# Late keys scored from transposed rows on TensorE, a swept input projection, a re-ordered bank queue and an interleaved cross-attention in a one-layer hybrid decoder step

## The reference, cut to what matters

```python
h = rmsnorm(x); q, k, v, u = split(h @ w_in)         # q,k,v: 8 heads x 64; u: 512 channels
# mixer A, prompt: dilated window attention among the 256 tokens, with a bias by distance
# mixer A, sample: 4 new queries against a cache of 2048 keys, three branches
#   (window, dilation) = (128,1), (512,4), (2048,16); branches merged by their softmax denominators
# mixer B: trailing means over 2/4/8/16 positions minus the token, one 128x128 map per group
x += concat(A, B) @ w_out
mk, mv = rmsnorm(mem) @ w_xk, rmsnorm(mem) @ w_xv    # 256 memory rows for the prompt
x += softmax(q_x @ keys) @ values @ w_xo             # 4 heads x 256; each sample has its own cached 256 rows
x += moe(rmsnorm(x))                                 # top 4 of 32 experts, each 1024 -> 2048 -> 1024
y = rmsnorm(x)                                       # and the caches, shifted by 4 rows, are outputs
```

## Time and profile before

| | |
|---|---|
| median of the runs | 1447.03 us (1445.16 to 1451.53, 3 runs) |
| the profiled execution | 1451.07 us, of which its span is 1449.3 us |
| mean granted TensorE clock | 0.953 of full speed |
| busy, us | PE 1274.4, PEld 530.7, DVE 479.3, ACT 238.5, POOL 67.2 |
| moved by DMA | 562.83 MB, mean 388 GB/s |
| the chain that ended last | DMA 49%, PE 38%, DVE 10%, issue 1%, ACT 1% |

### The profile page before, as it was taken

The page is one execution under the profiler, slowest core; times in us unless marked ns, Lnnn a source line. Parts: engine busy times, 40 slices in busy tenths (PEclk is TensorE's granted clock), DMA queues, the critical chain, the costliest instruction groups (busy, mean ns, idle before and its releaser), DMA issues.

```text
span 1449.3 us, 16480 instructions
## 1 busy us (share of the span) xinstructions
PE 1274.4 (88%) x6397; PEld 530.7 (37%) x6397; DVE 479.3 (33%) x1020; ACT 238.5 (16%) x467; POOL 67.2 (5%) x69
## 2 busy tenths in 40 slices
PE   7985978899779799999999899899998999989996
PEld 4352333347554433333333333333332333333332
DVE  2038989631413523122221231213212222123124
ACT  2135343220221111100010011011010001001102
POOL 1010000002202400000000000000000000000000
PEclk9985988799999699999999999999999999999999
DMA  9979698799989999999999999999999999999993
GB/s 352 360 257 365 252 384 349 290 352 377 339 311 391 336 395 430 427 428 426 427 429 430 429 427 429 430 428 428 428 428 430 428 427 428 430 429 427 428 428 141
DMA packets 51212, 562.83 MB, mean 388 GB/s; under 512 B 6501, under 2 KB 8645, under 8 KB 20349
## 3 DMA queue, kind: packets, MB, share of 16 engines
q1 hardware_dynamic: 49589, 557.16, 94.1%
q0 software_dynamic: 1584, 5.13, 0.9%
HBM read 556.15 MB, written 73.28 MB: 434 GB/s over the span
## 4 chain that ended last, share of the span: by engine, by line
DMA 49%; PE 38%; DVE 10%; issue 1%; ACT 1%; SPq 0%; DVEq 0%
DMA wide<-in_w_gate_up 48%; PE bank L1816 11%; PE bank L1511 3%; PE bank L1400 3%; PE bank L1532 3%; PE bank L1845 2%; PE bank L1554 2%; PE bank L1618 2%; DVE small L1120 2%; DVE wide L1117 1%; PE bank L1416 1%; DMA wide<-in_cache_mem_k 1%; PE bank L1669 1%; DVE wide L1118 1%; PE bank L1798 1%
## 5 line engine op out<-in xcount | busy, mean ns | idle before, releaser
L1816 PE MATMUL bank<-wide,att 128*64 128x512 f32 x2048 | 463.7, 596 | 60.5 <-DMA wide<-in_w_gate_up 60.3
L1816 PEld LDWEIGHTS bank<-wide,att 128*64 128x64 f32 x2048 | 139.1, 136 | 365.1 <-issue 228.0
L1845 PE MATMUL bank<-slim,att 128*64 128x512 f32 x1024 | 226.8, 595 | 0.0
L1322 DVE TENSOR_SCALAR att<-bank 128x512 f32<-128x512 f32 x32 | 22.1, 691 | 471.4 <-PE bank L1816 471.4
L1845 PEld LDWEIGHTS bank<-slim,att 128*64 128x64 f32 x1024 | 70.6, 137 | 152.2 <-issue 149.2
L1301 DVE TENSOR_TENSOR x<-x,bank 128x512 f32<-128x512 f32 x68 | 46.6, 685 | 233.0 <-PE bank L1798 226.4
L920 ACT ACTIVATE att<-att 128x512 f32<-128x512 f32 x32 | 20.2, 630 | 520.0 <-DVE att L1322 520.0
L1798 PE MATMUL bank<-tb,att 128*128 128x512 f32 (+1 forms) x192 | 84.7, 611 | 1.8 <-issue 1.3
L929 ACT ACTIVATE tb<-bank 64x512 f32<-64x512 f32 x64 | 37.8, 591 | 234.1 <-PE bank L1845 233.7
L1532 PE MATMUL bank<-slim,ta 128*128 128x512 f32 x128 | 58.2, 608 | 0.0
L1120 DVE TENSOR_REDUCE small<-wide 128x24 f32<-128x1536 f32 x32 | 56.1, 1753 | 1.1
(11 more groups left out here) (271 smaller groups left out, 1131.8 us busy)
## 6 DMA issues: line engine op xcount, KB each, us to landing
wide<-in_w_gate_up SPq DMA_DIRECT2D x128, 2048.0 KB, 25.5
slim<-in_w_down SPq DMA_DIRECT2D x64, 2048.0 KB, 22.0
out_k_win_sample<-in_cache_k_win SPq DMA_DIRECT2D x16, 2044.0 KB, 24.3
out_v_win_sample<-in_cache_v_win SPq DMA_DIRECT2D x16, 2044.0 KB, 29.0
wide<-in_cache_k_win SPq DMA_DIRECT2D x16, 1024.0 KB, 9.6
wide<-in_cache_v_win SPq DMA_DIRECT2D x16, 1024.0 KB, 6.8
wide<-in_w_in SPq DMA_DIRECT2D x8, 1024.0 KB, 14.8
wide<-in_cache_mem_k SPq DMA_DIRECT2D x8, 1024.0 KB, 19.7
```

The lines of the kernel that those rows point to most:

```text
L1816: ins = M(bk[half[h], :], rows[:, k, :], wide[:, k, c:c + 512], start=False, stop=k == KC - 1)
L1845: ins = M(bank_y[half[h], :], aT[:, f % 4, f // 4, :], slim[:, f, 512 * h:512 * h + 512], start=f == 0, stop=f == KC - 1)
```

## The change

It has four parts that share one diff.

**Late keys.** Slot 8 is no longer multiplied on DVE. TensorE transposes it (job `trl b`), ACT evicts it (`lateT`), TensorE multiplies it with `qd`, in which each query stands in its own head's 64 rows and zeroes elsewhere (job `sl b`, four matmuls of 8 columns), and DVE adds the bias from PSUM straight into the score tile. DVE builds `qd` once.

**Projection sweep.** `u` and tile 0's q, k, v are done together chunk by chunk in seven banks; then the bias products, `state`, the eight `toep`, `qkv 2`, `utp`, `uts`, and last tile 1. ACT and DVE follow in that order, so that the trailing sums come while tile 1 is multiplied.

**Re-ordered queue.** SP loads `x` before `ident` and `gcol`, and the weights before the bias constants. The first key and value windows wait for job `qkv 1 2` and no longer stand behind the load of `diag`, which waits for `stored["pool"]`. `COPIES` is now 6 and 4 around the bias load, 2 after the windows, 1, 0, 1, 1, 1 in the loop, 2 after it, 2 behind the cached memory keys, then 5, 2, 2 as before, and 3 instead of 6 behind the first expert's `w_gate_up`.

**Cross-attention.** `qm` is zeroed before the residual and filled one `xq` job at a time. The list `CROSS` interleaves the sample keys and scores with the prompt units; `xpt 3` and `xo_ 3` come after `xpts`.

```diff
-        add("bias_w"), add("bias_f")
+        for c in range(4):
+            add("u", c)
+        for c in range(3):
+            add("qkv", 0, c)
+        add("bias_w"), add("bias_f"), add("state")
+        for h in range(HEADS):
+            add("toep", h)
+        add("qkv", 2), add("utp"), add("uts")
+        for c in range(3):
+            add("qkv", 1, c)
...
-        COPIES = [7, 2, 1, 1, 1, 1, 1, 1, 2, 5, 2, 2, 6]
+        COPIES = [6, 4, 2, 1, 0, 1, 1, 1, 2, 2, 5, 2, 2, 3]
...
-            add("qb", b, 2), add("pt", b)
+            add("qb", b, 2), add("sl", b), add("pt", b)
...
+            if b + 1 < DEC_B:
+                add("trl", b + 1)
...
+        CROSS = [("keys", 2), ("scores", 1), ("xs", 0), ("keys", 3), ("scores", 2), ("xs", 1), ("xpt", 0), ("keys", 4), ("scores", 3),
+                 ("xo_", 0), ("keys", 5), ("scores", 4), ("xs", 2), ("xpt", 1), ("keys", 6), ("scores", 5), ("xo_", 1), ("keys", 7),
+                 ("scores", 6), ("xs", 3), ("scores", 7), ("xpt", 2), ("xo_", 2)]
...
 # SP
-            sp.wait_ge(stored["pool"], 48)
-            load(sp, "diag", own, i["c_diag"])
-            b, use = place(("u", 3))
+            b, use = place(("qkv", 1, 2))
             sp.wait_ge(bank_full[b], use + 1)
             window(kwin[0], i["cache_k_win"], 0, k_in[0])
             window(vwin, i["cache_v_win"], 0, v_in)
             window(kwin[1], i["cache_k_win"], 1, k_in[1])
+            sp.wait_ge(stored["pool"], 48)
+            load(sp, "diag", own, i["c_diag"])
...
 # ACT, after the fills of a turn
+            def late_turned(b):
+                ps, s = product(act, "trl", b)
+                if b:
+                    b_, use = place(("sl", b - 1))
+                    act.wait_ge(bank_full[b_], use + 1)
+                A(lateT, ps[:, :].rearrange("p (c n) -> p c n", n=P), ACT.Copy).then_inc(s, 1)
...
 # DVE, in the loop over b and t
-                dve.wait_ge(late_k, b + 1)
-                    V.tensor_tensor(prod[:, 0:2, :], pair, ps[:, :].unsqueeze(1).broadcast_to([P, 2, AW]), ALU.mult)
-                    V.tensor_tensor(prod[:, 2, :], kw[:, 8, :], ps[:, :], ALU.mult).then_inc(s, 1)
+                    V.tensor_tensor(prod, pair, ps[:, :].unsqueeze(1).broadcast_to([P, 2, AW]), ALU.mult).then_inc(s, 1)
-                    link(V.tensor_reduce(S_[b % 2][:, :, t, :], prod.rearrange("p k (h d) -> p k h d", d=HD), AX.X, ALU.add))
+                    link(V.tensor_reduce(S_[b % 2][:, 0:2, t, :], prod.rearrange("p k (h d) -> p k h d", d=HD), AX.X, ALU.add))
                     if b and t < 3:
                         (shift, sums, shares)[t](b - 1)
+                    if t == 2:
+                        ps, s = product(dve, "sl", b)
+                        V.tensor_tensor(S_[b % 2][:, 2].rearrange("p t (c h) -> p c t h", h=2),
+                                        ps[:, 0:32].rearrange("p (c t h) -> p c t h", c=4, h=2),
+                                        bsw[:, 2].rearrange("p t (c h) -> p c t h", h=2), ALU.add).then_inc(s, 1)
...
 # TensorE: row(b, 2), then late_scores(b), then turned(b); late_turn(b + 1) after the fills
+            def late_turn(b):
+                pe.wait_ge(late_k, b + 1)
+                ps, s = take(pe, "trl", b)
+                for c in range(4):
+                    ins = TR(ps[:, P * c:P * c + P], kwin[b % 2][:, 8, P * c:P * c + P], ident[:, :])
+                ins.then_inc(s, 1)
+            def late_scores(b):
+                read_out(pe, "trl", b)
+                ps, s = take(pe, "sl", b)
+                for c in range(4):
+                    ins = M(ps[:, 8 * c:8 * c + 8], lateT[:, c, :], qd[:, c, 8 * b:8 * b + 8], start=True, stop=True)
+                ins.then_inc(s, 1)
...
 # DVE, qm
-            for b in range(DEC_B):
-                ins = V.tensor_copy(qm.rearrange("p (c b n) -> p c b n", c=KC, b=DEC_B)[:, :, b, DEC_T * b:DEC_T * b + DEC_T],
-                                    tb[:, :, SEQ + DEC_T * b:SEQ + DEC_T * b + DEC_T])
+            for c in range(8):
+                read_out(dve, "xq", c)
+                V.tensor_copy(qm[:, QB * c:QB * c + QB].rearrange("p (b n) -> p b n", b=DEC_B)[:, :, 0:DEC_T],
+                              tb[:, c, SEQ:T].rearrange("p (b t) -> p b t", t=DEC_T)).then_inc(qm_in, 1)
```

More of the change, by code:

```diff
@@ L730, in _, with rows_out @@
                 root(t, n, x[0:n, t, :], hn[0:n, t, :])
[L732 to L735, removed]
+            def rows_out(t):
                 for c in range(3):
@@ L738, in _ @@
                     A(qkvn[:, c, t, :], ps[:, :], ACT.Copy, scale=HD ** -0.5 if c == 0 else 1.0).then_inc(s, 1)
-            ps, s = product(act, "qkv", 2)
-            for c in range(3):
-                ins = A(qkvn[0:NS, c, 2, :], ps[NS * c:NS * c + NS, :], ACT.Copy, scale=HD ** -0.5 if c == 0 else 1.0)
-            ins.then_inc(s, 1)
             for c in range(4):
@@ L747, in _ @@
                 A(uS[:, c, :, STATE:US], ps[:, SEQ:T].rearrange("p (b t) -> p b t", t=DEC_T), ACT.Copy).then_inc(s, 1)
+            rows_out(0)
+            ps, s = product(act, "state")
+            A(uS[:, :, :, 0:STATE], ps[:, 0:480].rearrange("p (g b n) -> p g b n", g=4, n=STATE), ACT.Copy).then_inc(s, 1)
+            for h in range(HEADS):
+                ps, s = product(act, "toep", h)
+                A(toep_sb[h // 5][:, h % 5, :], ps[:, 0:TOEP], ACT.Copy).then_inc(s, 1)
+            ps, s = product(act, "qkv", 2)
+            for c in range(3):
+                ins = A(qkvn[0:NS, c, 2, :], ps[NS * c:NS * c + NS, :], ACT.Copy, scale=HD ** -0.5 if c == 0 else 1.0)
+            ins.then_inc(s, 1)
+            ps, s = product(act, "utp")
+            A(hn[0:STATE, 2, 0:512], ps[0:STATE, :], ACT.Copy).then_inc(s, 1)
+            ps, s = product(act, "uts")
+            A(hn[0:NS, 2, 512:1024], ps[0:NS, :], ACT.Copy).then_inc(s, 1)
+            read_out(act, "qkv", 2)
+            b_, use = place(("qkv", 1, 2))
+            act.wait_ge(bank_full[b_], use + 1)
             for c in range(3):
@@ L1073, in _ @@
             logits(0)
+            read_out(dve, "trq", 2)
+            link(V.memset(qd, 0.0))
+            for h in range(2):
+                r = slice(64 * h, 64 * h + 64)
+                ins = V.tensor_copy(qd[r].rearrange("p c (n h) -> p c n h", h=2)[:, :, :, h], qT[r, :, SEQ:T])
+            ins.then_inc(qd_in, 1)
             for t in range(2):
@@ L1191, in xmax, with xshare @@
                 V.tensor_reduce(stat[:, c:c + 2], ps[:, :].rearrange("p (h n) -> p h n", n=NMEM), AX.X, ALU.max, negate=True).then_inc(summed, 1)
[L1193 to L1196 removed]
+            def xshare(u):
                 read_out(dve, "xs", u)
@@ L1670, in _ @@
                 ins.then_inc(s, 1)
+            pe.wait_ge(qm_in, KC)
+            cross_scores(0)
+            for kind, n in CROSS:
+                if kind == "keys":
+                    turn_keys(n)
+                elif kind == "scores":
+                    cross_scores(n)
+                elif kind == "xs":
+                    xscores(n)
+                elif kind == "xpt":
+                    xturned(n)
+                else:
+                    xvalues(n)
             pe.wait_ge(xprob, 2)
```

296 lines of the change are left out of this document (155 added, 141 removed).

## The result

The changed kernel took 1463.41 us (median of 4, 1459.92 to 1468.03), against 1448.43 us before on the same chip: ratio 1.0104, 95% interval 1.0087 to 1.0121. It is 1% slower; I had forecast 0.8% faster. The profiled execution took 1459.92 us with a span of 1458.1, 8.8 over the span before, where the sum had said 11.0 under it.

A forecast was written before the change was run, and what follows sets the result against it. It took the end as the expert stream's start plus a constant, with a TensorE-ACT-DVE ring pacing the sample loop. Terms +0.7 (to the loop's end), -6.4 and -5.3 gave -11.0: 1436 us against 1447.03, 8-in-10 range 1421 to 1450.

The forecast's parts named there:

- The step that failed: First window: idle time absorbs 20 us of three more copies, so the first product comes 5.9 us earlier than 120.92.
- rival 4: The gains don't arrive: first window lands behind ten copies and the backlog saved is idle anyway; 1447, chance 0.14.
- The backlog: Expert stream's start: 8 to 9 us of queued DMA work, removed by three copies fewer behind the first expert; -5.3 kept.
- The cross-attention: From `xq` to the expert's pieces: interleaving helps TensorE, but `xdiag` is held up behind `w_xo` and two copies; -6.4 us.
- Rival 2: Cross-attention: `xdiag` isn't held up, because fewer bytes are ahead of it than counted; eight more, 1428, chance 0.13.
- The loop: Sample loop: three late turns at +1.85 and a last one at +1.0 make it 6.6 us longer.
- +1.85 a turn: Late sample-loop turns: +2.2 for the late keys' work, -1.2 for DVE's cut, +0.85 for query rows between shares and values.
- about cancel: Streams 0 to 2 of the sample loop: DVE's cut (4.9 us a stream) and the new chain through ACT offset each other.
- rival 1: DVE sets the sample loop's pace: four turns at -1.8 instead of +1.65 give 14 us more; 1422, chance 0.19.
- Rival 3: Sample loop's fills run partly at half clock: 3.5 us a turn over seven fills, 24 us; 1460, chance 0.12.
- The clock of the values: Sample loop: values' matmuls stay at half clock (1.2 GHz); at 2.4 GHz they would take 2.7 us less a turn.
- the ring: Sample loop: a closed chain of waits through TensorE, ACT and DVE sets its pace, 20.2 us a turn.

The follow-up runs named there:

- e6: Kernel before with only its copy numbers made those of the changed kernel (ten ahead of the first windows, three behind the first expert); 1461.62 us, ratio 1.0081.
- e11: Kernel before, copy numbers alone: seven ahead of the windows, three more in the first streams, none ahead of `xdiag`, three behind the first expert; 1452.23 us, ratio 1.0037.
- e5: Changed kernel, copies alone: one instead of four before the first windows, three more in streams 0 to 2, the two ahead of `xdiag` behind it; 1442.86 us, ratio 0.9957.
- e1: Changed kernel with three of the ten copies ahead of the first windows put back behind the first expert; 1457.07 us, ratio 1.0045.
- e3: Changed kernel with three early copies put back behind the first expert and the two ahead of `xdiag` moved behind it; 1454.28 us, ratio 1.0044.
- e10: Changed kernel with the copies of e5 and the late keys' scores back on DVE as in e4; 1431.57 us, ratio 0.9890.
- e2: Changed kernel with the two copies between `w_xo` and `xdiag` moved behind `xdiag`; 1448.03 us, ratio 0.9994.
- e4: Changed kernel with the late keys' scores alone back on DVE (product over slot 8); 1456.32 us, ratio 1.0038.
- e7: Changed kernel with DVE's addition of the late scores moved from the third to the second query; 1454.18 us, ratio 1.0051.
- e9: Changed kernel with the copies of e5 and the early addition of e7, but the cross-attention's interleaving undone; 1447.12 us, ratio 0.9995.

## Why the prediction was wrong

Two pairs of runs part the code from the copies. With the change's copies, its code makes no difference that can be told: 1461.62 (e6) and 1463.41. (The numbers are the same there, the places not quite: in e6 the windows also stand behind `diag`.) With good copies the code is worth 9 us: 1452.23 (e11) and 1442.86 (e5). The change's copies cost the kernel before 13 us; good ones take 20 off the changed kernel. The mechanisms that I named for the code were mostly there; the transfers decided.

**The step that failed** is in the paragraph on the first window: "Three more make 20 us, which the idle time of that stage about absorbs." It was wrong by 10.1 of the 19.8 us. The first half of the step held: `qkv 1 2` was full at 100.37 (99.3 forecast). But the copies didn't run off in idle time, they held up what came next, twice. `toep`'s load waited until 86.55, not for TensorE or ACT, which were done by 70.3, but for the store of the bias products: issued at 71.45 behind six copies, it landed 15.1 us later (5.1 before, and 5.1 in e1 with three copies ahead). Four more copies, queued behind that load, so went out only at 87 to 89.5, right ahead of the windows (in e1 at 76.7 to 79.2). The window landed 24.27 us after its issue, DVE stood idle 7.5 us. I had counted copies against the idle time of the stage; what counts is the bytes outstanding when the window, or the store, is issued. With one copy there instead of four, and the six others where they were, the first product is at 116.13 (e5), though `toep`'s load still goes out at 85.59; so the four copies are what delays the window. The forecast of 115 was nearly right for a window that isn't held up, and I had only priced a held-up window as a gain lost (rival 4), never as a loss.

**The backlog** (-5.3 forecast, -2.1 measured). The sign held, the size didn't: I reckoned with 8 to 9 us of backlog and kept 5.3 of it without working that out, and the kernel before had about 2.3 to give. It can be read from the time between TensorE's first release to the second expert (the issue of its first pieces) and the end:

| kernel | first release | end of the span | between |
|---|---|---|---|
| before | 505.54 | 1449.3 | 943.8 |
| changed | 516.56 | 1458.1 | 941.5 |
| e1, six copies behind the expert | 511.58 | 1453.1 | 941.5 |
| e3, six, and four behind `xdiag` | 495.08 | 1450.8 | 955.7 |
| e5 | 498.59 | 1439.9 | 941.3 |
| e10 | 487.38 | 1429.1 | 941.7 |

In the changed kernel and all of e1 to e11 but e3 it is 941.3 to 941.9, wherever the copies stand. There TensorE's first release alone sets the end. So the empty DMA engines from 500 to 516 aren't a loss of their own, they are what a late release looks like from the queue. Only before (2.3 us over the rest) and e3 (14.2 over) wait for bytes as well:

```profile
495.08 14.68 SPq L601 DMA_DIRECT2D wide<-in_w_gate_up  x4
```

The end is the later of the two, as the forecast said; what it had wrong is how much the bytes held back in the kernel before.

**The cross-attention** (-6.4 forecast, +0.9 measured). The mechanism I named is what happened: `xdiag` held up behind `w_xo` and two copies, 15.97 us. Three sizes were off. `xq` took 34.33 us instead of 31.3, because it began at 1.2 GHz (the granted clock is 0.50 from 340 to 344 and 0.64 from 344 to 348). No instruction of the change stands there, but whether the change has a part in it is open: `xq` took 33.3 to 34.4 us in all seven profiled kernels with late keys on TensorE that didn't wait for `w_xq` in it. `pvxt` took 6.99 us; before, it was 3.69. TensorE had waited 10.62 us for the masks just ahead of it, and the granted clock was 0.50 from 437 to 446 (1.00 before, from 431.5 to 435.2). In e2, where that wait was 1.17, `pvxt` took 4.6; in e1, e4 and e7, where `xdiag` is held up too, 6.99. So the held-up load cost a second time, through the clock, 3.3 us. The third is the late scatter told below. The interleaving itself is worth more than I gave it (e9), once `xdiag` doesn't cap it. Rival 2 had priced that at eight more, but for another reason, fewer bytes ahead of `xdiag` than counted, and that one didn't come true: they were there, and held it up.

**The loop** (+6.6 forecast, +4.6 measured). The sign was right, the places not. In the late streams I had +1.85 a turn; it was 63.1 - 60.7 = 2.4 us for three, 0.8 a turn. The part of 0.85 for the rows behind `sl`'s bank was there and measured 1.2 (e7, 3.5 us in three turns). The rest, 2.2 put on less 1.2 taken off, came to nothing: e7 takes 59.6 us for these turns and e4, without late keys on TensorE, 59.55. Most of that is a term that I had put at nothing, the clock of the values (below): their matmuls are 0.9 us a turn shorter in e7 than in e4. In the early streams I wrote that cut and new chain "about cancel". They don't: against e4 the first turn is 2.1 us longer and the way to the first values 1.4, since TensorE is the limit there. That DVE sets the pace (rival 1) is refuted by e4. Rival 3 gave 1460, the right number for the wrong reason: but for the first (8.45 us, before 8.30) the fills took 7.13 us as before. Its mechanism does exist, at a fraction of its price: in e1, e2, e5 and e9 one more fill took 8.6 to 8.8 us, in e5 with a granted clock of 0.66 from 161.7 to 166. That happened in four of the eight profiled kernels with late keys on TensorE and in none of the five without.

**The clock of the values.** The forecast left it where it was. It moved. The sixth of the eight values, first in the changed kernel, then in e4, without late keys on TensorE:

```profile
262.12 4.17 PE L1611 MATMUL bank<-wide,pr 128*32 128x512 f32 x24
...
255.75 5.35 PE L1596 MATMUL bank<-wide,pr 128*32 128x512 f32 x24 [1.89 <-DVE pr L1126]
```

The granted clock over them is 0.66 in the one and 0.50 in the other. The fifth to seventh values took 3.8 to 4.7 us in all eight profiled kernels with late keys on TensorE, and 5.2 to 5.35 in all five without (the kernel before, e4, e6, e10, e11). In the changed kernel this gives back 0.9 to 1.2 us a turn. The page "TensorE: Matmul & The Clock Gate" of the Trainium skill (Part 4: PE-mode transpose) says that transposes don't count as busy time in the same way, and the forecast took from it that the late transposes bring no faster clock. The late work does bring one; but it is the transposes, the score matmuls and other waits together, and no run parts them, so the page's rule is neither confirmed nor refuted.

Open: why the clock at the start of `xq` and `out` stands at 1.2 GHz in some executions and not in others. It was 3 us at `xq`. Executions of one kernel differ by up to 14 us (e1: 1448.32 to 1462.20); how much of that is the clock wasn't separated.

## What to carry to other kernels

When a kernel ends in a long stream of weights, draw two clocks: the bytes that must have moved by the time the stream begins, and the moment at which buffers are released. The later one sets the end. Moving filler transfers forward pays only where the bytes are later (e11 gained nothing by it), and an earlier release only as far as the bytes have moved (e3). Filler goes where the DMA engines are idle and nothing urgent follows within its length; count what is outstanding when the urgent load is issued, and ask of every small load and store that others wait for (`xdiag`, `diag`, the store of the bias products) whose bytes stand ahead of it. Before taking work off a busy engine, look in each stage whose idle gap it would shorten; here taking 39 us of work off DVE made the loop 8 us longer, since TensorE and the ring had to carry what replaced it.

## What the runs showed of the hardware

A tiny DVE copy can wait out a GpSimd instruction. The eight scatters of `qm` (128x32, SBUF to SBUF) take 0.18 us each where nothing holds them, but in the changed kernel the last two:

```profile
368.57 8.19 POOL L677 TENSOR_TENSOR att<-att 32x2048 f32<-32x2048 f32 x2 [7.94 <-issue]
...
371.66 1.00 DVE L1221 COPY att<-tb 128x32 f32<-128x32 f32 x1 [3.70 <-ACT tb L890]
...
375.54 1.25 DVE L1221 COPY att<-tb 128x32 f32<-128x32 f32 x1 [2.88 <-ACT tb L890]
...
376.85 1.07 PE L1707 MATMUL bank<-att 128*32 128x256 f32 x16 [1.79 <-DVE att L1221]
```

The last ends at 376.79, when GpSimd's pair of subtractions ends (368.57 + 8.19 = 376.76), the one ahead of it at 372.66, halfway through the pair, and TensorE waits 1.79 us for the last. In e2, with the pair at 375.53, the two took 3.25 and 3.50 us. In the kernel before, the eight in a row took 4.71 us beside the same GpSimd work, where eight times 0.18 is 1.5. In e10 the same subtractions begin later, and nothing is stretched:

```profile
359.59 0.18 DVE L1206 COPY att<-tb 128x32 f32<-128x32 f32 x1 [3.70 <-ACT tb L885]
359.82 1.07 PE L1687 MATMUL bank<-att 128*32 128x256 f32 x16 [0.72 <-DVE att L1206]
...
362.02 1.50 DVE L1199 COPY att<-bank 128x512 f32<-128x512 f32 x2 [2.26 <-PE bank L1664]
362.11 8.23 POOL L675 TENSOR_TENSOR att<-att 32x2048 f32<-32x2048 f32 x2 [10.85 <-issue]
```

DVE's copy out of PSUM (L1199) isn't stretched by the same instruction beside it. The page "SBUF — State Buffer" of the Trainium skill (section "SBUF: two separate sides") says that DVE and GpSimd share a pair of ports under an exclusive lock, which GpSimd, or a DVE instruction in a mode that uses two ports or with two SBUF inputs, holds for its whole instruction if it starts first. The rows agree with it, by their end times; no run moved GpSimd's work on purpose.
